# Activations' high and low parts side by side, one 512-column matmul for both, in a hybrid encoder block

## What is computed

```python
xn = rmsnorm(h, norm1_g); proj = xn @ w_in            # 47 tiles of 128 columns
y = concat(ssd(...), sliding_window_attention(...))    # mixed heads, normalised
h = h + y @ w_out                                      # 16 tiles
xn = rmsnorm(h, norm2_g)
q  = (xn @ w_q).reshape(t, 8, 2, 128)                  # 16 tiles of queries
sc = einsum("thpk,hpnk->thpn", q, keys)                # scores against 2 x 128 keys a head
s1, i1 = top_k(sc[:, :, 0], 16); s2, i2 = top_k(sc[:, :, 1], 16)
top, pos = top_k(s1[..., None] + s2[..., None, :], 16) # 16 of 256 pairs a token and head
eidx = take(i1 * 128 + i2, pos); gate = softmax(top)
act = gelu(einsum("thkd,td->thk", u_tab[eidx], xn))    # 16384 experts, 16 chosen a head
h = h + einsum("thk,thkd->td", gate * act, v_tab[eidx])
out = rmsnorm(h, norm_f_g)
```

## Time and profile before

| what | value |
|---|---|
| median of 3 runs | 1964.51 us (1964.34 to 1965.58) |
| profiled execution | 1963.53 us, its span 1961.7 us |
| PE busy, share of the span | 96% |
| DVE, ACT, POOL busy | 61%, 46%, 23% |
| lines 1149 to 1151 (256 columns) on the chain that ended last | 18% each |
| lines 1344 to 1348 (512 columns) on that chain | 12% each |

### The profile page before, as it was taken

One profiled execution on the slowest core, in us unless ns is written; L12 is line 12 of the kernel. 1 busy time (PEld: TensorE's weight loads), 2 busy tenths in 40 slices (PEclk: granted clock), 3 DMA queues, 4 the chain that ended last, 5 costly groups with the idle time before them and its releaser, 6 DMA issues.

```text
span 1961.7 us, 37176 instructions
## 1 busy us (share of the span) xinstructions
PE 1885.6 (96%) x12738; PEld 1742.9 (89%) x12738; DVE 1194.6 (61%) x2125; ACT 893.5 (46%) x1153; POOL 451.1 (23%) x265
## 2 busy tenths in 40 slices
PE   3899997999999999999999999999999999999998
PEld 3897887999999999999999999888888888888886
DVE  6877777665888889443434343555555555555554
ACT  4243463444446666643434444444444444444443
POOL 2200000000003777787777750000000000000000
PEclk8899998999999999999999999999999999999999
DMA  4443354888656777777777765676666666666663
GB/s 142 139 161 119 117 162 126 264 272 259 216 182 178 184 173 192 178 187 187 178 187 177 186 179 189 228 259 218 216 219 215 219 214 219 215 221 214 219 215 121
DMA packets 166688, 379.77 MB, mean 194 GB/s; under 512 B 49920, under 2 KB 82816, under 8 KB 166400
## 3 DMA queue, kind: packets, MB, share of 16 engines
q1 hardware_dynamic: 129792, 379.25, 58.1%
q0 software_dynamic: 36864, 0.15, 5.1%
HBM read 358.22 MB, written 21.10 MB: 193 GB/s over the span
## 4 chain that ended last, share of the span: by engine, by line
PE 91%; DVE 4%; ACT 1%; issue 1%; DVEq 0%; ACTq 0%
PE ps L1149 18%; PE ps L1150 18%; PE ps L1151 18%; PE ps L1344 12%; PE ps L1348 12%; PE ps L1346 12%; DVE low L636 1%; DVE big L756 0%; PE ps L1215 0%; PE ps L1204 0%; ACT high L415 0%; PE ps L1374 0%; DVE big L646 0%; PE ps L1315 0%; DVE big L783 0%
## 5 line engine op out<-in xcount | busy, mean ns | idle before, releaser
L636 DVE TENSOR_TENSOR low<-raw,high 128x1024 fp32r<-128x1024 f32 x638 | 775.1, 1232 | 633.9 <-ACT high L415 631.0
L1149 PE MATMUL ps<-act_hi,high 128*128 128x256 f32 x3056 | 874.9, 286 | 48.8 <-DVE low L636 34.3
L1150 PE MATMUL ps<-act_lo,high 128*128 128x256 f32 x3056 | 869.5, 285 | 0.0
L1151 PE MATMUL ps<-act_hi,low 128*128 128x256 f32 x3056 | 869.2, 284 | 0.0
L415 ACT ACTIVATE high<-raw 128x1024 fp32r<-128x1024 f32 x638 | 656.7, 1054 | 458.6 <-PE ps L1348 378.8
L1149 PEld LDWEIGHTS ps<-act_hi,high 128*128 128x128 f32 x3056 | 591.6, 194 | 58.9 <-issue 31.4
L1150 PEld LDWEIGHTS ps<-act_lo,high 128*128 128x128 f32 x3056 | 591.7, 194 | 0.1
L1151 PEld LDWEIGHTS ps<-act_hi,low 128*128 128x128 f32 x3056 | 591.4, 194 | 0.0
L401 POOL DMA_INDIRECT gate_scratch<-gates_sb,cells_sb x256 | 427.9, 1671 | 676.6 <-DVE gates_sb L1068 553.2
L1344 PE MATMUL ps<-high,w_hi 128*128 128x512 f32 x1024 | 315.5, 389 | 1.3 <-ACT big L420 1.3
L1348 PE MATMUL ps<-high,w_lo 128*128 128x512 f32 x1024 | 315.2, 389 | 0.0
(11 more groups left out here) (155 smaller groups left out, 665.7 us busy)
## 6 DMA issues: line engine op xcount, KB each, us to landing
raw<-u_tab SPq DMA_DIRECT2D x256, 512.0 KB, 3.2
raw<-v_tab SPq DMA_DIRECT2D x256, 512.0 KB, 3.2
raw<-w_in SPq DMA_DIRECT2D x62, 512.0 KB, 3.7
raw<-w_out SPq DMA_DIRECT2D x32, 512.0 KB, 5.1
gate_scratch<-side SPq DMA_DIRECT2D x32, 512.0 KB, 6.7
raw<-w_q SPq DMA_DIRECT2D x32, 512.0 KB, 5.6
side<-gate_scratch SPq DMA_DIRECT2D x128, 128.0 KB, 3.4
gate_scratch<-gates_sb,cells_sb POOLq DMA_INDIRECT x256, 4.5
```

Source lines behind the costliest of these rows:

```text
L636: V.tensor_tensor(slot(low, s), slot(raw, s), slot(high, s).bitcast(F32), ALU.subtract).then_inc(lo_done, 1)
L1149: mm(acc, wh, a_hi, start=(kk == 0), stop=False)
L1150: mm(acc, wh, a_lo, start=False, stop=False)
L1151: ins = mm(acc, wl, a_hi, start=False, stop=(kk == KT - 1))
```

## The change

The activation tiles `act_hi` and `act_lo` (and `act2_hi`, `act2_lo`) become one tile each, `act1` and `act2`, in which the high and the low part of a 256-column tile lie side by side. A new PE function `paired` takes the place of `product` in queries and first table. For each of the 16 tiles it issues one matmul of 512 columns (high weights by both parts) and one of 256 (low weights by the high part). The bank then holds two halves that must be added:

- ACT copies the second half to SBUF (`take_half`, into `half_t`), and DVE adds it to the first (`add_halves` in the first table, two instructions in `query_step`).
- Gelu becomes an instruction of its own on ACT, after DVE's sum: `gelu(c-1)` stands in `expert_step(c)` between `cut_high(c+1)` and `take_half(c)`. The semaphores `half_ok`, `gelu_ok` and `query_ok` are new.
- A routing step on DVE goes with four chunks, and in it every second half-cut is followed by `add_halves` of the chunk two before. The softmax goes in eight batches of two routing steps.

```diff
-ROUTE_SPAN = 3
+ROUTE_SPAN = 4
-ROUTE_BATCHES = 4
+ROUTE_BATCHES = 8
...
+            def take_half(c, par, dst):
                 act.wait_ge(used, 2 * c + 2)
-                nc.scalar.activation(dst, ps[:, par, 0:T], func).then_inc(taken, 1)
+                nc.scalar.activation(dst, ps[:, par, T:2 * T], ACT.Copy).then_inc(half_ok, 1)
...
             def query_step(m, j):
+                if not (isinstance(m, int) and m < 2):
+                    act.wait_ge(score_ok, m - 1)
+                take_half(C_WQ + m, (C_WQ + j) % 2, q_t[j])
...
-            def expert_step(c, par):
+            act.wait_ge(cleared, 16 * (N_KEYS // ZERO_CHUNKS))
+            def gelu(c):
+                act.wait_ge(taken, c + 1)
+                cell = big[:, ds((c - C_U) * T, T)]
+                nc.scalar.activation(cell, cell, ACT.Gelu).then_inc(gelu_ok, 1)
+            def expert_step(c, par, first=False):
                 cut_high(c + 1, 1 - par)
-                at = (c - C_U) * T
-                take(c, par, big[:, ds(at, T)], ACT.Gelu)
+                if not first:
+                    gelu(c - 1)
+                take_half(c, par, half_t[par])
...
             expert_step(C_V_TAB - 1, (C_V_TAB + 1) % 2)
+            gelu(C_V_TAB - 1)
...
             def query_step(m, j):
-                take(C_WQ + m, (C_WQ + j) % 2, q_t[j], rs_r[:, 0:T])
+                dve.wait_ge(half_ok, m + 1)
+                V.tensor_tensor(q_t[j], ps[:, (C_WQ + j) % 2, 0:T], q_t[j], ALU.add).then_inc(taken, 1)
+                dve.wait_ge(taken, C_WQ + m + 1)
+                V.tensor_tensor(q_t[j], q_t[j], rs_r[:, 0:T], ALU.mult).then_inc(query_ok, 1)
...
+            def add_halves(e, par):
+                dve.wait_ge(half_ok, 2 * PEER_HEADS + e + 1)
+                V.tensor_tensor(big[:, ds(e * T, T)], ps[:, par, 0:T], half_t[par], ALU.add).then_inc(taken, 1)
             def route(i, rr):
                 def cut(n):
-                    k = ROUTE_SPAN * rr + 1 + n // 2
+                    k = ROUTE_SPAN * rr + 2 + n // 2
                     cut_low_piece(C_U + 2 * ROUTE_SPAN * i + k, (C_U + k) % 2, n % 2)
+                    if n % 2:
+                        add_halves(2 * ROUTE_SPAN * i + k - 2, (C_U + k) % 2)
...
-                    if k == 1:
-                        cut(0)
+                    if k < 3:
+                        cut(k)
                     own.settle()
-                cut(1)
+                cut(3)
...
+            def paired(c, par, ins, ready=None):
+                pe.wait_ge(taken, c - 1)
+                acc = ps[:, par, :]
+                for half in range(2):
+                    s = 2 * par + half
+                    pe.wait_ge(lo_done, 2 * c + half + 1)
...
+                    for k in range(8):
+                        kk = 8 * half + k
+                        both = ins[:, kk * 2 * T:(kk + 1) * 2 * T]
...
+                        if kk < KT - 1:
+                            mm(acc, wh, both, start=(kk == 0), stop=False, skip_group_check=True)
+                        ins_mm = mm(acc[:, 0:T], wl, hi_of(ins, kk), start=False, stop=False, skip_group_check=True)
+                        if kk == KT - 1:
+                            ins_mm = mm(acc, wh, both, start=False, stop=True, skip_group_check=True)
+                    ins_mm.then_inc(used, 1)
```

More of the change, by code:

```diff
@@ L120, in build @@
         with ExitStack() as early:
-            act_hi = sb(early, "act_hi", KT * T, F32R)
-            act_lo = sb(early, "act_lo", KT * T, F32R)
+            act1 = sb(early, "act1", KT * 2 * T, F32R)
             gates_sb = sb(early, "gates_sb", ROUTE_STEPS * TOPK)
@@ L137, in view, with hi_of, lo_of, quarter @@
             return big[:, at:at + cols]
+        def hi_of(t, k):
+            return t[:, ds(k * 2 * T, T)]
+        def lo_of(t, k):
+            return t[:, ds(k * 2 * T + T, T)]
+        def quarter(t, q, part):
+            return t.rearrange("p (k s t) -> p k s t", s=2, t=T)[:, 4 * q:4 * q + 4, part, :]
+        def four(t, q):
+            return t[:, q * 4 * T:(q + 1) * 4 * T].rearrange("p (k t) -> p k t", t=T)
         x_sb, h_sb, y_sb, sq_sb, xn_sb = (view(a, KT * T) for a in (X_T, H_T, Y_T, SQ, XN))
@@ L260, in build @@
         mix_ok = sem("mix_ok")
+        half_ok = sem("half_ok")
+        gelu_ok = sem("gelu_ok")
+        query_ok = sem("query_ok")
         score_ok = sem("score_ok")
@@ L428, in round_norm @@
                     act.wait_ge(xn_ok, 4 * k + q + 1)
-                    a, b = q * 4 * T, (q + 1) * 4 * T
-                    nc.scalar.activation(act_hi[:, a:b], xn_sb[:, a:b], ACT.Copy).then_inc(xh_ok, 1)
+                    nc.scalar.activation(quarter(act1, q, 0), four(xn_sb, q), ACT.Copy).then_inc(xh_ok, 1)
             round_norm(0)
@@ L539, in round_tile @@
             def round_tile(m, dst, src):
-                nc.scalar.activation(dst[:, ds(m * T, T)], src[:, ds(m * T, T)], ACT.Copy).then_inc(tile_hi, 1)
+                nc.scalar.activation(hi_of(dst, m), src[:, ds(m * T, T)], ACT.Copy).then_inc(tile_hi, 1)
             def out_step(m, j):
@@ L562, in query_step @@
                 act.wait_ge(tile_ok, KT + m + 1)
-                round_tile(m, act_hi, y_sb)
-            with act.Fori(0, KT // 2 - 1) as i:
+                round_tile(m, act1, y_sb)
+            for m in range(2):
+                query_step(m, m)
+            with act.Fori(1, KT // 2 - 1) as i:
                 for j in range(2):
@@ L960, in _ @@
             score_take(KT - 1, 1)
-            tile_low(KT - 1, 2 * KT - 1, act_hi, act_lo)
+            tile_low(KT - 1, 2 * KT - 1, act1)
+            cut_low(C_U + 1, (C_U + 1) % 2)
             dve.wait_ge(score_out, 2 * PEER_HEADS)
@@ L1011, in route @@
                     if k == 1:
-                        cut(2)
+                        cut(4)
                     own.settle()
-                cut(3)
+                cut(5)
                 own.step(V.tensor_scalar(r_ab[0], r_tp, 4, None, ALU.logical_shift_right))
@@ L1025, in route @@
                         "p (o a) -> p o a", o=1).broadcast_to([P, TOPK, TOPK]), ALU.mult))
-                cut(4)
+                cut(6)
                 own.settle()
@@ L1029, in route @@
                     own.step(V.tensor_reduce(big[:, ds(PICKS + s * 256 + r * TOPK, TOPK)], r_eq[s], AX, ALU.add))
-                cut(5)
+                cut(7)
                 own.settle()
@@ L1084, in cut_pairs @@
                     for j in range(2):
-                        cut_low(C_U + 1 + 2 * i + j, (C_U + 1 + j) % 2)
+                        cut_low(C_U + 2 + 2 * i + j, (C_U + j) % 2)
+                        add_halves(2 * i + j, (C_U + j) % 2)
             cut_pairs(ROUTE_CHUNKS, ROUTE_CHUNKS + 4)
             share(ROUTE_BATCHES - 1)
-            cut_pairs(ROUTE_CHUNKS + 4, N_KEYS)
+            cut_pairs(ROUTE_CHUNKS + 4, N_KEYS - 2)
+            cut_low(C_V_TAB, C_V_TAB % 2)
+            for e in range(N_KEYS - 2, N_KEYS):
+                add_halves(e, (C_U + e) % 2)
             def weights(e, par, between):
                 dve.wait_ge(gate_back[par], 8 * (e + 2 - (par - C_V_TAB) % 2))
-                dve.wait_ge(taken, C_U + 1 + e)
+                dve.wait_ge(gelu_ok, e + 1)
                 gelu = big[:, ds(e * T, T)]
@@ L1131, in _, with product @@
             mm = nc.tensor.matmul
-            def product(c, par, midway=None, ins_hi=None, ins_lo=None, ready=None):
+            def product(c, par, midway=None, ready=None):
                 if not (isinstance(c, int) and c < 2):
@@ L1154, in product @@
                         midway()
+            def paired(c, par, ins, ready=None):
[4 more added lines that the diff above has]
+                    pe.wait_ge(lo_done, 2 * c + half + 1)
+                    if ready:
+                        pe.wait_ge(ready[0], ready[1 + half])
+                    for k in range(8):
+                        kk = 8 * half + k
+                        both = ins[:, kk * 2 * T:(kk + 1) * 2 * T]
+                        wh = high[:, s * PIECE + k * P:s * PIECE + (k + 1) * P]
+                        wl = low[:, s * PIECE + k * P:s * PIECE + (k + 1) * P]
+                        if kk < KT - 1:
[4 more added lines that the diff above has]
+                    ins_mm.then_inc(used, 1)
             def sum_tiles(bank, lo, tiles, src, start=True, stop=True):
@@ L1302, in _ @@
                     product(C_OUT + 2 * i + j, (C_OUT + j) % 2)
-            query = dict(ins_hi=act2_hi, ins_lo=act2_lo)
-            product(C_WQ, C_WQ % 2, ready=(tile_lo, KT // 2, KT), **query)
+            paired(C_WQ, C_WQ % 2, act2, ready=(tile_lo, KT // 2, KT))
             pe.wait_ge(h_summed, 1)
@@ L1319, in _ @@
             for j in range(2):
-                product(C_WQ + 1 + j, (C_WQ + 1 + j) % 2, **query)
+                paired(C_WQ + 1 + j, (C_WQ + 1 + j) % 2, act2)
                 scores(j, j)
@@ L1323, in _ @@
                 for j in range(2):
```

(10 more changed lines are left out.)

37 lines of the change are left out of this document (16 added, 21 removed).

## The result

| | before | after |
|---|---|---|
| median | 1964.42 us (1964.04 to 1965.58, 4 runs) | 2023.88 us (2021.94 to 2027.57, 4 runs) |
| profiled execution, span | 1961.7 us | 2023.6 us (time 2025.42) |
| ratio | | 1.030, 95% interval 1.029 to 1.032 |

What follows compares the result with a forecast made beforehand. PE's matmuls bound the kernel; after the change an ACT-DVE circle with table loads would hold PE up. From 1963.5 us, less 27.2 and 3.4, plus 79, 0.8 and 1.0: 2013.7, put as 2013 us; range 1998 to 2028.

Steps and rivals of the forecast that it cites:

- Nothing but the circle makes PE wait: First table: ACT and DVE wait for each other in turn, one turn a chunk; PE waits where turns exceed 5.558 us.
- The 79 us: First table: PE's waiting, 424.4 us for 62 turns against PE's 344.6, less about 1 us in hand.
- The circle, 4.61 us, and one load a turn, 5.91: First table: one turn through ACT and DVE takes 4.61 us, and 5.91 with a table load of 1.30.
- Routing pieces between the cuts, 0.84 us a chunk; those behind the sum, nothing: DVE while routing: pieces between a chunk's two cuts add 0.84 us a turn; those between sum and next cut, nothing.
- 1.57 us a softmax: ACT in the first table: each of eight softmaxes holds it another 1.57 us, 12.6 us in all.
- The 62 turns take 424.4 us: First table, steps 9 to 71: 54 turns of 6.75 us, 8 of 5.91, plus 12.6 us of softmaxes.
- A chunk takes PE 5.558 us: First table: 16 tiles of 346.7 ns plus 0.011 us, against 5.771 before; 27.2 us less over 128 chunks.
- The queries: Query chunks: 16 chunks save 3.4 us, the end costs 0.8 us more; -2.6 in all.
- The end of the first table, 1.0 us more: Gap on PE between the tables: 2.27 us after, 1.29 before, through the added sum and separate Gelu.
- The front, 0: From the start to the root ahead of the queries: no change predicted.
- no loads in the loops: Rival: loops keep Gelu's table, the circle takes 5.45 us, only softmaxes cost, about 10 us: 1946 us; chance 0.12.
- The wide matmul saves nothing: Rival: 66 chunks outside the circle's waits and 16 query chunks lose 0.213 us each, 17.5 us: 2030 us; chance 0.08.

Runs made afterwards that it cites:

- the sum first: Changed kernel with DVE adding the halves ahead of the two low cuts, in `route` and `cut_pairs`, all table loads kept: 1951.9 us, ratio 0.993.
- four fewer: Changed kernel with four softmax batches of four routing steps instead of eight of two: 2007.0 us, ratio 1.021.
- the run without Exp: Changed kernel with the softmax's Exp replaced by Copy in `soften`: 1948.6 us, ratio 0.992.
- two wide and two narrow matmuls in turn: Changed kernel with DVE's addition ahead of the cuts, and PE doing two wide matmuls, then two narrow ones: 1946.7 us, ratio 0.991.
- four and four: Changed kernel with DVE's addition ahead of the cuts, and PE doing four wide matmuls, then four narrow ones: 1945.3 us, ratio 0.990.
- the run with the cuts together: Changed kernel with the first cut of a chunk moved behind the routing pieces, next to the second, in routing: 1979.2 us, ratio 1.007.
- Gelu brought back: Changed kernel with Exp kept and an extra Gelu of one column behind each Exp: 1970.4 us, ratio 1.003.

## Why the prediction was right

The forecast was 2013 us and slower; 2023.9 was measured, inside the range. The prediction's own sum, 2013.7 for the profiled execution and 1.0 more for the median, gives 2014.7 and not 2013. The spans differ by 11.7 us more than its terms (61.9 for 50.2), and nearly every term erred to the same side. By its steps:

- *Nothing but the circle makes PE wait.* Right: with the sum first PE waits for no sum, with the same instructions. The 79 us were called waiting, though, and only part is. From the start of PE's matmuls, 62 chunks under the circle take 358 us and some 66 us lie between them (the profile shows 56.0, since the modelled end of a matmul overlaps each gap). PE was 13 us slower than forecast there, some 6.5 of it in four falls of its clock; as the circle set the pace, nearly all of that took the place of waiting.
- *The circle, 4.61 us, and one load a turn, 5.91.* Right, within 0.06 us. Behind routing, a body of two chunks with its loads takes 11.70 us, from 961.25 to 972.95, 5.85 a chunk:

```profile
961.25 1.28 ACT L595 ACT_TABLE_LOAD   x1 [1.90 <-DVE big L1013]
...
972.95 1.28 ACT L595 ACT_TABLE_LOAD   x1 [1.90 <-DVE big L1013]
```

- *Routing pieces between the cuts, 0.84 us a chunk; those behind the sum, nothing.* Right: 44.7 us for 54 chunks when they are moved, 0.83 each, with some 0.05 of noise.
- *1.57 us a softmax.* Right: the turn with a softmax takes 9.41 us where the same turn without takes 7.9. In the sum, four fewer, with eight chunks out of the loops with loads, gave 16.9 where 6.3 and 10.4 were due.
- *The 62 turns take 424.4 us.* Their `take_half` instructions span 423.7 us in the trace of after, from step 9 to step 71.
- *A chunk takes PE 5.558 us.* The step that was mis-sized. It nearly does so in the first ten chunks (544.76 to 567.09 for four, 5.58), but behind routing it is 5.653, in the changed kernel too: 1103.69 to 1188.49 for 15. The 56 chunks behind the circle lose 0.095 each and the ten ahead of it 0.02, 5.5 us, nearly the whole miss in the first table (57.5 for 51.8). At 5.653 the wide matmul saves 0.118 us of the 5.771 before, not 0.213: of the 27.2 us on paper some 12 would be lost over all 128 chunks. That is also why the run without Exp came out 5 us too high: with the circle's waits gone, its chunks take 5.638 on average.
- *The queries.* Measured from the root, -1.2 for -2.6. The chunks lie 6.00 us apart, 6.20 before, and save 2.8 over fourteen intervals; a stall behind the first of them, where PE waits for the low part of the next (424.88), takes 0.5 back; and from the start of the last chunk's scores to the first table PE needs 2.42 us for 1.22, so the end costs 1.2 and not 0.8. ACT's last-but-one `take_half` stood behind a `cut_high` that waited for a transfer of the first table, which I had not counted among what is queued ahead of it. The last `take_half` is some 0.4 us late by what follows from it (509.23, 0.6 behind PE's scores at 508.61; within the loop it is 0.2), which is the difference:

```profile
503.69 1.06 ACT L429 ACTIVATE high<-raw 128x1024 fp32r<-128x1024 f32 x1 [0.20 <-DMA raw<-u_tab]
504.65 0.37 ACT L434 ACTIVATE big<-ps 128x256 f32<-128x256 f32 x1
...
509.23 0.36 ACT L434 ACTIVATE big<-ps 128x256 f32<-128x256 f32 x1
```

- *The end of the first table, 1.0 us more.* Right by itself (0.9), but PE's clock fell behind that gap, and the second table's first matmuls ran at half pace: 1.7 us that were priced at nothing. The prediction counted nothing for the clock because it had stayed up in the scan's stretch. Whether it falls at this place is luck, as the last section shows.
- *The front, 0.* Most of its 3.0 us isn't the change's: over twelve profiled executions, two with the front of before and ten with that of after, the root ahead of the queries starts between 415.6 and 419.1 us, and the one of after is the last of them. The two start at 416.1 and 416.7, the ten at 417.3 on average, so a few tenths may be the change's. It is a stretch with many gaps in which the granted clock differs from one execution to the next.

Of the rivals, "no loads in the loops" was priced at 1946 us with the softmax loads kept. The run without Exp took those away too; by the same prices that is 10 us less, 1936, and it took 1948.6. Of the 12.6 us between them 10 are the pace of a chunk (5.638 for 5.558, 128 times). "The wide matmul saves nothing" was half true: 0.118 us a chunk of 0.213.

## What to carry to other kernels

When a step that one engine did alone is shared between two, draw the order of both queues as a circle and sum one turn; where the turn is longer than the bounding engine's time, what stands on it counts in full, table loads and unrelated work between included, and here what stood beside it was free. The first thing to try is the order: the short instruction that releases others goes ahead of the long ones. Here that is worth 72 us and turns a loss of 3.0% into a gain of 0.7%, with two wide and two narrow matmuls in turn 0.9%.

A function in front of a loop can cost a table load in every round of it: see which table the loop is entered with.

## What the runs showed of the hardware

- A chunk of 16 wide and 16 narrow matmuls takes 5.56 us in some stretches and 5.65 in others, at a granted clock of 1.00 in both, and without PE waiting (in the run without Exp both values alternate while routing, and only 5.65 stands behind it). Two and two, or four and four, give 5.60. What decides isn't known; the three narrow matmuls of before had no such two values (5.74 to 5.78 from one `take` to the next behind routing).
- After a gap of 2.2 us on PE its clock can fall from the upper to the lower level (2.4 to 1.2 GHz), as at the start of the second table. In these rows of the chain that ended last, of after (start, us, two matmuls each), a pair takes up to 0.85 us there and 0.46 some us later:

```profile
1309.38 0.70 PE ps L1401 x2
1310.08 0.65 PE ps L1403 x2
1310.73 0.85 PE ps L1405 x2
...
1313.97 0.46 PE ps L1401 x2
```

Such a gap doesn't always do it. All ten profiled executions with the wide matmul have this same gap ahead of the second table, and the clock fell in six: from its first matmul to the end of the span these take 714.2 us, the other four 712.6. In the first table of after PE waits 2.2 to 2.3 us at seven of the eight softmaxes, and the clock fell at four of them, the first two, the sixth and the seventh. Two waits of 2.31 us, at 630.39 and at 741.29, with the stretch around each (granted clock third from the right):

```profile
630.39 0.49 PE L1208 MATMUL ps<-act,high 128*128 128x512 f32 x1 [2.31 <-DVE big L1013]
741.29 0.49 PE L1208 MATMUL ps<-act,high 128*128 128x512 f32 x1 [2.31 <-DVE big L1013]
630.00:637.00 7.00, 6.61 (x29) 5.65 (x30) 5.56 (x19) 3.86 (x5) 6.09 (x4) 0.76 0.64 157
741.00:748.00 7.00, 5.81 (x32) 4.84 (x32) 5.55 (x20) 3.87 (x5) 6.09 (x4) 1.00 0.69 166
```

Behind a fall the next turn takes 5.81 to 5.88 us instead of 5.49, so the circle hides all but 0.3 to 0.4 of it. No clock fell at the gaps of 1.2 us: from 594 to 622 us it is 1.00, and in the run with the cuts together, whose longest wait in the first table is 1.7 us, it never fell there. What decides between a gap with a fall and one without isn't known.
- A table load costs what it lasts: the instruction behind it starts 1.30 us after it, at both loads of the softmax with Gelu brought back (565.86 to 567.16, 567.40 to 568.70). The Trainium skill, "ScalarE: Activation LUTs", section "What ACT_TABLE_LOAD costs", gives the same 1283 ns for the load and adds 1380 ns of drain to each switch; these rows show no such addition.
